# Down projection of a conv FFN: block differences by a negating copy and an accumulating DMA instead of VectorE

## The reference, cut to what matters

```python
def conv_ffn(h, w_up, conv_w, w_down):
    s = h.shape[1]
    up = h @ w_up
    upp = jnp.pad(up, ((0, 0), (CONV_WIDTH - 1, 0), (0, 0)))
    conv = sum(upp[:, i:i + s] * conv_w[i] for i in range(CONV_WIDTH))
    gate, val = conv[..., :D_FF], conv[..., D_FF:]
    return (jax.nn.gelu(gate, approximate=True) * val) @ w_down
...
        x = x + rms_norm(conv_ffn(h2, w_up, conv_w, w_down), ln_post_ffn)
```

## Time and profile before

| | |
|---|---|
| median of 3 runs | 1600.33 us (1600.12 to 1600.61) |
| the profiled execution | 1600.68 us, span of its trace 1598.9 us |
| TensorE busy | 1589.9 us (99%), granted clock 0.999 |
| VectorE busy | 1221.4 us (76%) |
| ScalarE busy | 821.1 us (51%) |
| GpSimd busy | 2.0 us, 12 instructions |
| down projection | about from 1250 us to the end |

### The profile page before, as it was taken

One profiled execution on the slowest core, in us unless ns is written; L12 is line 12 of the kernel. 1 busy time (PEld: TensorE's weight loads), 2 busy tenths in 40 slices (PEclk: granted clock), 3 DMA queues, 4 the chain that ended last, 5 costly groups with the idle time before them and its releaser, 6 DMA issues.

```text
span 1598.9 us, 24334 instructions
## 1 busy us (share of the span) xinstructions
PE 1589.9 (99%) x8673; PEld 1377.3 (86%) x8673; DVE 1221.4 (76%) x1777; ACT 821.1 (51%) x1119; POOL 2.0 (0%) x12
## 2 busy tenths in 40 slices
PE   9999999999999999999999999999999999999998
PEld 8888888888888888888888888888888888888886
DVE  6556677677766787777777777777777899979996
ACT  6544544456555654444444444444444656566663
POOL 0000000000000000000000000000000000000000
PEclk9999999999999999999999999999999999999999
DMA  9885455546565465656556565565655565546552
GB/s 369 268 230 185 159 184 171 171 158 210 193 255 193 149 210 184 192 184 200 185 184 190 185 200 186 184 189 185 200 186 184 210 232 190 210 160 235 203 192 79
DMA packets 234947, 313.17 MB, mean 196 GB/s; under 512 B 5360, under 2 KB 209808, under 8 KB 234000
## 3 DMA queue, kind: packets, MB, share of 16 engines
q1 hardware_dynamic: 231056, 306.44, 58.2%
q10 hardware_dynamic: 3840, 6.05, 1.5%
HBM read 309.58 MB, written 2.88 MB: 195 GB/s over the span
## 4 chain that ended last, share of the span: by engine, by line
PE 99%; DVE 0%; ACT 0%; issue 0%; DVEq 0%
PE ps L1445 44%; PE ps L1449 23%; PE ps L1536 20%; PE ps L1782 5%; PE ps L1584 3%; PE ps L1549 1%; PE ps L1460 1%; PE ps L1465 0%; PE ps L1673 0%; PE ps L1654 0%; PE ps L1606 0%; PE ps L1666 0%; PE ps L1683 0%; PE ps L1731 0%; DVE arena L1421 0%; PE ps L1489 0%
## 5 line engine op out<-in xcount | busy, mean ns | idle before, releaser
L837 DVE TENSOR_TENSOR w_lo<-raw,w_hi 128x1024 fp32r<-128x1024 f32 x464 | 557.4, 1222 | 243.3 <-ACT w_hi L428 240.4
L428 ACT ACTIVATE w_hi<-raw 128x1024 fp32r<-128x1024 f32 x462 | 478.0, 1057 | 513.3 <-PE ps L1445 261.1
L1445 PE MATMUL ps<-actT,w_hi 128*128 128x512 f32 x3072 | 717.1, 390 | 0.0
L1445 PEld LDWEIGHTS ps<-actT,w_hi 128*128 128x128 f32 x3072 | 569.9, 188 | 114.1 <-issue 0.2
L1449 PEld LDWEIGHTS ps<-actT,w_lo 128*128 128x128 f32 x3072 | 383.4, 191 | 10.0 <-issue 1.7
L1449 PE MATMUL ps<-actT,w_lo 128*128 128x256 f32 x3072 | 389.4, 283 | 0.0
L1536 PE MATMUL ps<-w_hi,xs 128*128 128x512 f32 x944 | 255.4, 389 | 0.0
L1536 PEld LDWEIGHTS ps<-w_hi,xs 128*128 128x128 f32 x944 | 177.2, 188 | 36.7
L1536 PE MATMUL ps<-w_lo,xs 128*128 128x512 f32 x472 | 145.3, 389 | 0.0
L1249 DVE SCALAR_TENSOR_TENSOR arena<-arena,convw 128x256 f32<-128x256 f32 x256 | 106.8, 480 | 0.1
L1536 PEld LDWEIGHTS ps<-w_lo,xs 128*128 128x128 f32 x472 | 88.6, 188 | 18.4
(11 more groups left out here) (176 smaller groups left out, 881.4 us busy)
## 6 DMA issues: line engine op xcount, KB each, us to landing
raw<-in_w_up_dram SPq DMA_DIRECT2D x128, 1024.0 KB, 5.8
raw<-in_w_down_dram SPq DMA_DIRECT2D x64, 1024.0 KB, 5.2
raw<-in_w_in_dram SPq DMA_DIRECT2D x58, 1024.0 KB, 5.2
raw<-in_w_o_dram SPq DMA_DIRECT2D x16, 1024.0 KB, 5.2
raw<-in_w_a_out_dram SPq DMA_DIRECT2D x8, 1024.0 KB, 5.5
raw<-in_w_b_out_dram SPq DMA_DIRECT2D x8, 1024.0 KB, 5.5
arena<-in_x_dram SPq DMA_DIRECT2D x1, 2048.0 KB, 17.1
arena<-in_x_dram ACTq DMA_DIRECT2D x2, 1024.0 KB, 6.6
```

The lines of the kernel that those rows point to most:

```text
L428: act.activation(w_hi[:, h % RING, :], raw[:, h // 2, h % 2 * HALF:(h % 2 + 1) * HALF], ACT.Copy)\
L837: dve.tensor_tensor(w_lo[:, h % RING, :], raw[:, h // 2, h % 2 * HALF:(h % 2 + 1) * HALF], w_hi[:, h % RING, :].bitcast(F32), ALU.subtract ...
L1445: return pe.matmul(ps[:, bank + c, :], w_hi[:, h % RING, at:at + P], actT[:, k, :, :].rearrange("p a s -> p (a s)"), start=start, stop=stop)
```

## The change

ScalarE writes the negated first k-tile of the block, -B11 and -B12, into the first half of `yn[sweep]`. Pool's queue, idle before, then issues a DMA that reads B12 and B22 once more from `w_down` in device memory (512 KB) and adds them in flight to what stands there, which gives T1 and T3. Two new semaphores carry this: `negated` (ScalarE to Pool) and `added` (the DMA to ScalarE's L749 and VectorE's T2). VectorE's L1312 goes away. The negating copy stands between the halves j = 0 and j = 1 of its group, and waits for the block's load and, since it overwrites `yn`, for the last rest of the group before (`lo_ready`).

```diff
-        SUMS, HALVES_HI = 7, 7
+        SUMS, HALVES_HI = 6, 7
...
+            for sweep in range(2):
+                for g in range(GROUPS[sweep]):
+                    gr = Group(sweep, g)
+                    pool.wait_ge(negated, gr.forms + 1)
+                    cols = slice(sweep * SW + BLK, (sweep + 1) * SW)
+                    pool.dma_start(two(yn[sweep][:, 0, :]), w_down[:, gr.k + 4:gr.k + 6, cols], accum_op=ALU.add)\
+                        .then_inc(added, 16)
...
+            def negate(sweep, gr):
+
+                act.wait_ge(raw_landed[gr.slots[2]], gr.landed[2])
+                act.wait_ge(lo_ready, gr.before)
+                act.activation(yn[sweep][:, 0, :], raw[:, gr.slots[2], 0:2 * BLK], ACT.Copy, scale=-1.0).then_inc(negated, 1)
+
             def round_sums(sweep, gr):
 
                 n = SUMS * gr.forms
-                act.wait_ge(form_summed, n + 2)
+                act.wait_ge(added, 16 * gr.forms + 16)
                 act.activation(b_hi[:, BT:BT + 2 * BLK], yn[sweep][:, 0, :], ACT.Copy).then_inc(form_hi, 1)
...
             def down_group(sweep, gr):
 
                 for j in range(4):
+                    if j == 1:
+                        negate(sweep, gr)
...
                 dve.tensor_tensor(s1, a21, a22, ALU.add).then_inc(form_summed, 1)
-                dve.tensor_tensor(t13, quarters[:, :, 1, :], quarters[:, 0, :, :], ALU.subtract).then_inc(form_summed, 1)
                 dve.wait_ge(form_summed, n + 1)
                 dve.tensor_tensor(s2, s1, a11, ALU.subtract).then_inc(form_summed, 1)
                 dve.tensor_tensor(s3, a11, a21, ALU.subtract).then_inc(form_summed, 1)
+                dve.wait_ge(added, 16 * gr.forms + 16)
+                dve.tensor_tensor(t2, b22, yn[sweep][:, 0, 0:BLK], ALU.subtract).then_inc(form_summed, 1)
                 dve.wait_ge(form_summed, n + 2)
-                dve.tensor_tensor(t2, b22, yn[sweep][:, 0, 0:BLK], ALU.subtract).then_inc(form_summed, 1)
-                dve.wait_ge(form_summed, n + 3)
                 dve.tensor_tensor(s4, a12, s2, ALU.subtract).then_inc(form_summed, 1)
```

More of the change, by code:

```diff
@@ L262, in block_program @@
         form_lo = sem("form_lo")
+        negated = sem("negated")
+        added = sem("added")
         v_staged = sem("v_staged")
@@ L312, in att_base, with two @@
             return kv * sum(ATT) + n * ATT[0]
+        def two(v):
+            return v.rearrange("p (b c) -> p b c", b=2)
         block = ctx.enter_context(nc.Block())
@@ L743, in round_given @@
                 act.activation(a_hi[:, S:S + P], ffT[:, gr.k + 4, 0:P], ACT.Copy).then_inc(form_hi, 1)
+            def negate(sweep, gr):
+                act.wait_ge(raw_landed[gr.slots[2]], gr.landed[2])
+                act.wait_ge(lo_ready, gr.before)
+                act.activation(yn[sweep][:, 0, :], raw[:, gr.slots[2], 0:2 * BLK], ACT.Copy, scale=-1.0).then_inc(negated, 1)
             def round_sums(sweep, gr):
                 n = SUMS * gr.forms
-                act.wait_ge(form_summed, n + 2)
+                act.wait_ge(added, 16 * gr.forms + 16)
                 act.activation(b_hi[:, BT:BT + 2 * BLK], yn[sweep][:, 0, :], ACT.Copy).then_inc(form_hi, 1)
-                act.wait_ge(form_summed, n + 6)
+                act.wait_ge(form_summed, n + 5)
                 act.activation(s_hi[:, 0:3 * P], s123, ACT.Copy).then_inc(form_hi, 1)
                 act.activation(s_hi[:, 3 * P:4 * P], s4, ACT.Copy).then_inc(form_hi, 1)
-                act.wait_ge(form_summed, n + 7)
+                act.wait_ge(form_summed, n + 6)
                 act.activation(b_hi[:, BT + 2 * BLK:BT + 4 * BLK], yn[sweep][:, 1, :], ACT.Copy).then_inc(hi_ready, 2)
@@ L1127, in _ @@
                 y_turn(i)
-            def two(v):
-                return v.rearrange("p (b c) -> p b c", b=2)
             def sweep_out(bank, t, dst, gains, ready, count):
@@ L1302, in sum_forms @@
                 block = raw[:, gr.slots[2], :]
-                quarters = block.rearrange("p (a b c) -> p a b c", a=2, b=2)
-                t13, t2, t4 = two(yn[sweep][:, 0, :]), yn[sweep][:, 1, 0:BLK], yn[sweep][:, 1, BLK:2 * BLK]
+                t2, t4 = yn[sweep][:, 1, 0:BLK], yn[sweep][:, 1, BLK:2 * BLK]
                 b21, b22 = block[:, 2 * BLK:3 * BLK], block[:, 3 * BLK:4 * BLK]
@@ L1315, in sum_forms @@
                 dve.tensor_tensor(s3, a11, a21, ALU.subtract).then_inc(form_summed, 1)
+                dve.wait_ge(added, 16 * gr.forms + 16)
+                dve.tensor_tensor(t2, b22, yn[sweep][:, 0, 0:BLK], ALU.subtract).then_inc(form_summed, 1)
                 dve.wait_ge(form_summed, n + 2)
-                dve.tensor_tensor(t2, b22, yn[sweep][:, 0, 0:BLK], ALU.subtract).then_inc(form_summed, 1)
-                dve.wait_ge(form_summed, n + 3)
                 dve.tensor_tensor(s4, a12, s2, ALU.subtract).then_inc(form_summed, 1)
-                dve.wait_ge(form_summed, n + 5)
+                dve.wait_ge(form_summed, n + 4)
                 dve.tensor_tensor(t4, b21, t2, ALU.subtract).then_inc(form_summed, 1)
```

## The result

| | before | changed |
|---|---|---|
| median | 1600.27 us (4 runs) | 1618.3 us (4 runs, 1616.48 to 1620.15) |
| ratio | | 1.0112, 95% interval 1.0095 to 1.013 |
| profiled execution, span | 1600.68, 1598.9 | 1620.15, 1618.3 |
| granted clock | 0.999 | 0.996 |

What follows compares the result with a forecast made beforehand. TensorE, busy all 15.72 us of a group, was taken as the bound. Copy, removed instruction and traffic add 0; the DMA wait adds 4 x 7.0 - 22.4 = 5.6 us to 1600.68, median 0.35 lower: 1605.9, range 1600.0 to 1632.

Steps and rivals of the forecast that it cites:

- rival B: In every later group, copy, DMA and rests set the pace; L = 9.0 gives 27.9 us, 1628; chance 0.22.
- TensorE bounds, and VectorE's 19.4 us are worth nothing: TensorE is busy for all 15.72 us of a group; removing L1312, 17 times, gains 0 on the path.
- rival D: VectorE's freed 19.4 us come through, bounding TensorE somewhere unseen; at most 19 us, 1581; chance 0.03.
- The three places: First group, second group and every later group of a sweep, where the loss follows from L; 5.6 us at 7.0.
- the ring: Every later group: copy, DMA, sums and rests take L + 7.8 against TensorE's 15.72; above L = 7.9, L - 7.9 lost each.
- L: Time from the end of ScalarE's negating copy to `added`; not in the trace, taken as 7.0 us.
- L - 4.55 and L - 4.8: TensorE's stall before half j = 2 of the first group, in the first and second sweep.
- the same formula: Total loss over all groups of both sweeps for L above 7.9: 17L - 125.1 us.
- Traffic costs nothing by itself: 17 transfers of 512 KB have room on average; a load landing 1 or 2 us later costs nothing in middle groups.
- The copy costs 0: 17 copies on ScalarE, 1.05 us each; half j = 1 moves 1.7 us back, before TensorE needs it; cost 0.
- The second groups lose L - 6.5 each: Second group of each sweep: TensorE stalls L - 6.5 because the last rest comes late; 0.5 us expected.
- Rival C: Pool cannot issue its DMA while VectorE works; L would be 12 or more, 79 us, 1679; chance 0.06.

Runs made afterwards that it cites:

- both other causes removed: Changed kernel with two alternating buffers for T1 and T3, and VectorE's old instruction instead of copy and DMA in each sweep's first group: 1602.98 us.
- the run of the copy alone: Changed kernel without the DMA on Pool's queue: negating copy stays on ScalarE, VectorE adds B12 and B22 where L1312 stood: 1603.23 us, ratio 1.0015.
- two buffers: Changed kernel with T1 and T3 alternating between two buffers, so the negating copy no longer waits for the previous group's last rest: 1611.83 us, ratio 1.0066.

## Why the prediction was right or wrong

The prediction named the direction and two of the places, but its forecast of the loss was a third of what came: 5.6 us against 18, 1605.9 against 1618.3. The range contains the measured time only because it reached into rival B.

- **TensorE bounds, and VectorE's 19.4 us are worth nothing**: right. VectorE's busy time fell by 18 us and nothing became shorter; rival D is out.
- **The three places**: right in form. The first group's and the ring's sizes follow once L is put in. The first group's stall was given as L - 4.55 and L - 4.8. In the first sweep the copy ended at 1269.30 and T2 began at 1276.83, L = 7.5: 3.0 us, measured 3.07. In the second the DMA alone took 9.4 us; with 0.3 between copy and issue L is 9.7: 4.9 us, measured 5.10. The ring was given as L + 7.8; with the 8.28 above that is 16.08, measured 16.15.
- **L = 7.0**: this is the term that was mis-sized. It is 8.1 from issue to landing and some 0.3 more from the copy's end. The difference is 1.3 us, but it lies across the point at 7.9 where the slope goes from 4 to 17 us per us: at L = 8.3 the same formula gives 17 x 8.3 - 125.1 = 16.0, not 5.6. I took the middle between a load alone and a load in company, though SP's issues showed that it would have company in the middle groups; the row of 8.1 was the nearer one. L is not one number either: the DMA took 5.9 us to landing at one second group and 9.4 at one first. So rival B was what happened, and I had given it 0.22. That the corrected sum comes near the measured 18 us is partly luck. Its 16.0 are 7.2 for the first groups, 3.6 for the second and 5.2 for the ring; measured were 12.4, 0 and 7.2.
- **Traffic costs nothing by itself**: nearly right. SP's loads land 1.4 us later and nothing waits for them in a middle group. But traffic works on L itself, 2.2 us of it, and the 2.4 us that remain with both other causes removed are the two groups whose DMA landed late.
- **The copy costs 0**: wrong at the second group of a sweep. I followed its wait for L1348 in a middle group and not its wait for the block's load in the second, with three halves behind it. It cost 2.7 us in the run of the copy alone, but that run also keeps an addition on VectorE. Without one, in the run with VectorE's instruction only in the first groups, it cost no time of its own but 2.5 of the 3.2 us of slack there, which the ring then missed.
- **The second groups lose L - 6.5 each**: they lost nothing. Their own DMAs took 6.0 and 5.9 us, some 6.3 from the copy's end, with which the formula gives no loss either. VectorE came to T2 only after the DMA had landed, held up by the halves behind the copy, and TensorE, late by its clock as well, found its operands 1.8 and 2.2 us early.
- **What no term had**: the clock. At the first groups 12.4 us were lost, of which the waits before the half j = 2 are 8.2. The other 4.2 come after the restarts. From the rows above, as busy time times the missing share of the clock, 1.6 us of them are the clock's in the first sweep and 2.2 in the second; that is an estimate, since no run has the same wait without the fall of the clock.
- **Rival C**: out. Pool's row is 1.20 us beside a busy VectorE and beside an idle one. The Trainium skill (page SBUF — State Buffer, section Who interferes with whom) infers the same for `tensor_tensor`, that it does not hold up Pool's work on a DMA; these rows agree.
- **The two rules on L**: the fit of the Trainium skill's page DMA: Bandwidth & Descriptors (section Anatomy of one DMA) gives an estimate of 3.2 us, which is under the 4.2 us measured for a plain DMA alone. The Trainium skill's page Collectives: The Full Stack (section The bandwidth ceiling) says of a reducing DMA in a collective that its two reads halve the rate. The rates above, 213 against 369 GB/s, come near that; the time to landing is far from doubled, 5.9 us against 4.2.

## What to carry to other kernels

Work taken off an engine that is not waited for buys nothing, and what takes its place is a chain of latencies: follow it until it closes on itself, and compare its length with the period of the bounding engine, for past that point each group pays. Size an unseen DMA by the rows that have the company it will have, not by the mean of alone and together. When a long wait is put in an in-order queue, look at what stands behind it in the first and second pass of a loop, where the prefetch distance is shorter than in the middle: moving the wait behind two ready halves was worth 9 us here, with the ring already removed.

## What the runs showed of the hardware

- TensorE's granted clock went from 1.00 to 0.50 around single waits of 5.10, 4.46, 3.07, 2.42 and 2.12 us, and stayed at 1.00 with waits of 1.56 and 1.34. With the 5.10 us it was at 0.50 from before the restart at 1462.00 to 1466, so a part of the price comes after the wait, at some half of the matmuls of a full stretch.
- An accumulating DMA of 512 KB from Pool's queue took 5.9 us alone, 8.1 in the median beside the loads, and between 5.9 and 11.0 in single cases (with two buffers mostly near 6 and near 10 in turn; what decides between them was not tested); Pool's row for its issue was 1.20 us, against 0.72 for the plain one.
